# Subtracting the head means from the values instead of from the time mix's output, and a new order of the next stage's first products

## The chip, the cores and the metric

The kernel runs on one core of a Trainium2 chip. The metric is the device time of one execution in microseconds, and lower is better. All data is float32. The large products are split by hand into a high and a low half (`float32r`), so that each costs three passes of TensorE instead of one float32 product.

## The reference, cut to what matters

The program is two decoder layers for 512 tokens with a width of 1024. The change touches one branch of the first, an RWKV-7 time mix with 8 heads of 64 channels:

```python
def step(state, inp):
    r_t, w_t, k_t, v_t, kk_t, a_t = inp
    sa = einsum("bhvk,bhk->bhv", state, kk_t)
    state = (state * w_t[:, :, None, :] - sa[..., None] * (kk_t * a_t)[:, :, None, :]
             + v_t[..., None] * k_t[:, :, None, :])
    return state, einsum("bhvk,bhk->bhv", state, r_t)
...
mean = mean(out, axis=-1)                       # over the 64 channels of a head
var = mean(square(out - mean), axis=-1)
out = (out - mean) * rsqrt(var + GN_EPS) * lnx_w + lnx_b
bonus = sum(rh * kh * r_k, axis=-1) * vh        # with v itself
return (out + bonus) * g
```

The state is zero at first, and every channel v of `state`, `sa` and `out` is linear in the same channel of `v_t`. So if the mean over a head's 64 channels is taken off `v_t`, the output has no mean over them either. The bonus needs `v` as it is.

## The kernel before, in words

The kernel is a row of stages, each a block of five instruction streams (TensorE `pe`, ScalarE `act`, VectorE `dve`, GpSimd `pool`, and SyncE `sp` for DMA). Inside a stage the order of each stream is written out by hand and the streams meet only at semaphores; between stages all of them meet. Activations lie channel by token: a tile is 128 channels (partitions) by 512 tokens. Weights come in groups through two buffers: a DMA, a high part made by ScalarE (`split_hi`, L201), a low part by VectorE (`split_lo`, L209), and then three passes on TensorE (`product`, L232 to L234). An activation tile is split likewise (`Split.hi`, L297, on ScalarE; `Split.lo`, L303 without a gain and L305 with one, on VectorE).

Three stages matter.

The first, `proj_stage`, makes the projections. TensorE goes through 38 weight groups there, and `TimeMixIn.turn` (L499) puts twelve turns in between, two at a time: turns 0 to 3 bring the values `v` to token order, 4 to 7 the keys, 8 to 11 the rates. A turn is four transposes of 128x128 against the constant `ident`; ScalarE copies the result to SBUF.

The third, `time_mix_chunks_stage`, runs the recurrence in four chunks of 128 tokens, with the turned values, and leaves `out` (4 tiles). Its last instructions are a chain of short products and copies (L1201 to L1310).

The fourth, `front_region`, first finishes the time mix (`TimeMixOut`) and then merges three gated branches (`Gates`). The stream of TensorE in it is: `means` (four float32 products with `head_ones`, L1593), `variances` (four float32 products with 8 columns of weights, L1600), and then the loop over steps m = 0 to 35 of the first output tile, with `spread_out` (four float32 products over 8 rows, L1611) ahead of step 10; after that 7 more tiles in a hardware loop. A step is one `product`, so three passes. Steps 0 to 7 need the input tiles x0 to x7 in split form, steps 8 to 11 the branch tiles y0 to y3, steps 12 to 19 x again, steps 20 to 23 need y4 to y7, steps 24 to 31 x, and 32 to 35 need the split output r0 to r3. Nine steps use one weight group.

VectorE's stream at that place is: low parts of x0 and x1; `centre` of the four output tiles (L1624: subtracts the mean that `means` left in PSUM); low parts of x2 to x5; `variance` (L1633); the first `shift` (L1629); `invert` (a reciprocal, L1637, after ScalarE's square root L1620); low parts of x6, x7 and y0 to y3; `split_lo` of the third weight group (which needs step 8 done); and then for each output tile c: `shift`, `finish` (L1642, L1646, L1649), the low part of y(4+c), and the low part of r(c-1). `finish(c)` waits for the c-th product of `spread_out`.

ScalarE's stream: high parts of x0 to x3, four squares of the centred output (L1616), high parts of x4, x5, the square root, high parts of the rest.

Of the kernel before, what the change touches and what calls it, by code (L numbers as in the profile page):

```python
# [8 lines left out]
P = 128  # L9
# [6 lines left out]
NW = W // P  # L16
# [3 lines left out]
HD = 64  # L20
# [14 lines left out]
NEG = -1e30  # L35

ALU = mybir.AluOpType
# [32 lines left out]
for _name, _cols in VECS:  # L70
# [4 lines left out]

CONSTS = [
    ("ident", 128), ("ones", 128), ("head_ones", 128), ("upper", 128), ("causal4", 512), ("neg_tri", 128),
    ("neg_ones", 128), ("neg_diag_t", 128), ("level", 896), ("flip", 128),
    ("causal_add", 128), ("cmp_add", 124), ("cmp_keep", 124), ("head_cols", 32),
]  # L80
CONST_AT = {}
# [313 lines left out]
class TimeMixIn:  # L395
# [94 lines left out]
    def turn(self, pe, u):  # L490
        source, n = (self.v, self.k, self.rate)[u // 4], u % 4
        if u < 4:
            pe.wait_ge(self.bonus_ready, u + 1)
            pe.wait_ge(self.mixed, 14)
        else:
            pe.wait_ge(self.placed, u - 3)
            pe.wait_ge(self.k_made if u < 8 else self.b_made, NW)
        for c in range(NW):
            mm = pe.transpose(self.ps[:, n, c * P:(c + 1) * P], source[:, c, n * P:(n + 1) * P], self.core.c("ident"))  # L499
        mm.then_inc(self.turned, 1)  # L500


# [529 lines left out]
def head_spread(core):  # L1032

    return core.arena[0:HEADS, 70, :]
# [532 lines left out]
class TimeMixOut:  # L1567


    def __init__(self, core, ps):  # L1570
        a = core.arena
        self.core, self.ps = core, ps
        self.out, self.bonus, self.gate = a[:, 8:12, :], a[:, 30:34, :], a[:, 46:50, :]
        self.square, self.rstd = a[:, 56:60, :], a[0:HEADS, 60, :]
        self.spread, self.spread_in = head_spread(core), core.sem("to_spread_in")
        self.mean_banks, self.spread_banks, self.sum_bank = (0, 1, 6, 7), (1, 0, 7, 1), 0
        self.inverted, self.rstd_spread = core.sem("to_inverted"), core.sem("to_rstd_spread")
        self.mean_done, self.centred = core.sem("to_mean_done"), core.sem("to_centred")
        self.squared, self.var_done = core.sem("to_squared"), core.sem("to_var_done")
        self.var_ready, self.rooted = core.sem("to_var_ready"), core.sem("to_rooted")  # L1580
        self.shifted, self.scaled = core.sem("to_shifted"), core.sem("to_scaled")
        self.summed, self.gated = core.sem("to_summed"), core.sem("to_gated")
        self.gate_back, self.bonus_back = core.sem("to_gate_back"), core.sem("to_bonus_back")
# [4 lines left out]
        sp.dma_start(self.spread, self.core.dram["head_spread"]).then_inc(self.spread_in, 16)  # L1588
        sp.wait_ge(self.spread_in, 16)

    def means(self, pe):
        for c in range(NW):
            pe.matmul(self.ps[:, self.mean_banks[c], :], self.core.c("head_ones"), self.out[:, c, :], start=True, stop=True)\  # L1593
              .then_inc(self.mean_done, 1)

    def variances(self, pe):
        pe.wait_ge(self.centred, 1)
        for c in range(NW):
            pe.wait_ge(self.squared, c + 1)
            mm = pe.matmul(self.ps[0:HEADS, self.sum_bank, :], self.core.c("head_cols", c * HEADS, HEADS), self.square[:, c, :],  # L1600
                           start=(c == 0), stop=(c == NW - 1))
        mm.then_inc(self.var_done, 1)

    def spread_out(self, pe):
        pe.wait_ge(self.spread_in, 16)
        pe.wait_ge(self.inverted, 1)
        pe.wait_ge(self.centred, NW)
        for c in range(NW):
            if c == 3:
                pe.wait_ge(self.scaled, 1)  # L1610
            pe.matmul(self.ps[:, self.spread_banks[c], :], self.spread[:, c * P:(c + 1) * P], self.rstd, start=True, stop=True)\  # L1611
              .then_inc(self.rstd_spread, 1)

    def take_square(self, act, c):
        act.wait_ge(self.centred, c + 1)
        act.activation(self.square[:, c, :], self.out[:, c, :], ACT.Square).then_inc(self.squared, 1)  # L1616

    def root(self, act):
        act.wait_ge(self.var_ready, 1)
        act.activation(self.rstd, self.rstd, ACT.Sqrt).then_inc(self.rooted, 1)  # L1620

    def centre(self, dve, c):
        dve.wait_ge(self.mean_done, c + 1)
        dve.scalar_tensor_tensor(self.out[:, c, :], self.ps[:, self.mean_banks[c], :], -1.0 / HD, self.out[:, c, :], ALU.mult, ALU.add)\  # L1624
           .then_inc(self.centred, 1)

    def shift(self, dve, c):
        dve.wait_ge(self.bonus_back, 16)
# [23 lines left out]
class Gates:  # L1652
# [24 lines left out]
    def tensor(self, pe):  # L1677
        core, to = self.core, self.to

        def step(m, d=None):  # L1680
            n, k = m // 12, m % 12
            if k == 0:

                pe.wait_ge(self.pairs_free, n + 1 if d is None else d * 3 + n + 1)
            g = self.g0 + m // 9 + (0 if d is None else 4)
            if m % 9 == 0:
                core.wait_weights(pe, g, 0 if d is None else d - 1)
            if d is None and n == 0 and k < KD:
                pe.wait_ge(self.x_split.lowered, k + 1)
            elif d is None and k >= KD and n < 2:  # L1690
                pe.wait_ge(self.y_split.lowered, 4 * n + k - KD + 1)
            elif d is None and k >= KD:
                pe.wait_ge(to.scaled, NW)
                pe.wait_ge(self.r_split.lowered, k - KD + 1)
            w = core.weights(g, (m % 9) * P, (m % 9 + 1) * P)
            if k < KD:
                mm = product(pe, self.ps[:, 2 + 2 * n, :], w, self.x(k), k == 0, k == KD - 1)
            else:
                mm = product(pe, self.ps[:, 3 + 2 * n, :], w, self.branch(4 * n + k - KD), k == KD, k == 11)
            if m % 9 == 8:  # L1700
                mm.then_inc(core.groups_done, 1)

        to.means(pe)
        to.variances(pe)
        for m in range(36):
            if m == 10:
                to.spread_out(pe)
            step(m)
        with pe.Fori(1, KD) as d:
            for m in range(36):  # L1710
                step(m, d)
        core.used += 32

    def scalar(self, act):
        core, g0 = self.core, self.g0

        def merge(d):
            act.wait_ge(self.summed, 2 * (d + 1))
            act.activation(core.pair(XN_HI, XN_LO, d)[0], self.total[:, d % 2, :], ACT.Copy).then_inc(self.upper, 1)

        def open_up(d, n):
            act.wait_ge(self.logits_ready, 3 * d + n + 1)
            act.activation(self.open_gate[:, n, :], self.open_gate[:, n, :], ACT.Sigmoid, bias=core.v("gate_b", 8 * n + d))\
               .then_inc(self.opened, 1)

        to = self.to
        for k in range(4):
            self.x_split.hi(act, k)
        for c in range(NW):
            to.take_square(act, c)  # L1730
        for k in range(4, 6):
            self.x_split.hi(act, k)
        to.root(act)
        for k in range(6, KD):
            self.x_split.hi(act, k)
        for k in range(KD):
            self.y_split.hi(act, k)
        core.split_hi(act, g0 + 2)
        for c in range(NW):
            act.wait_ge(to.gated, c + 1)  # L1740
            self.r_split.hi(act, c)
            if c == 2:
                core.split_hi(act, g0 + 3)
        open_up(0, 0)
        core.split_hi(act, g0 + 4)
        open_up(0, 1)
        core.split_hi(act, g0 + 5)
        open_up(0, 2)
        for d in range(1, KD):
            for m in range(4):  # L1750
                core.split_hi(act, g0 + 4 * d + m + 2)
                if m:
                    open_up(d, m - 1)
                else:
                    merge(d - 1)
        merge(KD - 1)

    def vector(self, dve):
        core, g0, to = self.core, self.g0, self.to
# [19 lines left out]
                dve.tensor_tensor(total, total, result, ALU.add).then_inc(self.summed, 1)  # L1779

        dve.sem_inc(self.pairs_free, 3)
        for k in range(2):
            self.x_split.lo(dve, k)
        for c in range(NW):
            to.centre(dve, c)
        for k in range(2, 6):
            self.x_split.lo(dve, k)
        to.variance(dve)
        to.shift(dve, 0)
# [1580 lines left out]
def _constants():  # L3370
    c = {name: np.zeros((P, cols), np.float32) for name, cols in CONSTS}
    i = np.arange(P)
    row, col = i[:, None], i[None, :]
# [3 lines left out]
    c["upper"][:] = row <= col  # L3377
    c["causal4"][:] = np.concatenate([row < col, row <= col, row < col, row <= col], axis=1)
    c["neg_tri"][:] = -1.0 * (row >= col)
    c["neg_ones"][:] = -1.0  # L3380
    c["neg_diag_t"][:] = np.where(row < col, 0.0, NEG)
    for n in range(7):
        b = 1 << n
        c["level"][:, n * P:(n + 1) * P] = (col // b % 2 == 1) & (row // b == col // b - 1)
# [95 lines left out]
```

## Time and profile before

| | us |
|---|---|
| median of 3 runs | 2110.09 |
| lowest, highest | 2106.38, 2111.42 |
| profiled execution, from first to last instruction (its span) | 2103.3 |
| TensorE busy in it | 2021.3 |
| VectorE busy | 1079.6 |
| ScalarE busy | 800.6 |
| mean granted TensorE clock, 1 being full | 0.984 |

Of the profiled execution's own time the profile gives the span alone; the lowest run is 3.1 us above that span and the median 6.8 us. The profile shows TensorE busy for 96% of the span; the clock is granted at full speed nearly all of the time. Where such a kernel can gain or lose is in the few places at which TensorE stands idle, does work that could be left out, or runs at half its clock. The stretch that the change touches is small, so the timelines of a few engines over some 40 us say more than the shares of the whole.

### The profile page before, as it was taken

Reading aid. Unit: us, or ns where it says so; the run is one execution under the profiler, and the core shown is the slowest. Engines: PE = TensorE matmul, PEld = TensorE weight load, DVE = VectorE, ACT = ScalarE, POOL = GpSimd, SP = SyncE. Lnnn points to the kernel's source line nnn. Section 1 sums busy time; section 2 is a strip of 40 time slices with the busy share of each in tenths; the row PEclk is TensorE's granted clock in tenths of the full one; section 3 lists DMA queues with packets and bytes.
Section 4 is the critical chain, followed back from the end, with each engine's and each line's share of the span. In section 5 each row is a group of like instructions: output and inputs, shape, how many; then the busy total and the mean of one; then the engine's idle time right before and its main releaser. Section 6 shows DMA issues by size and latency. Waiting matters only on the chain. (4 is left out here: it accounts for less than half of the span.)

```text
span 2103.3 us, 29578 instructions
## 1 busy us (share of the span) xinstructions
PE 2021.3 (96%) x11736; PEld 1611.2 (77%) x11736; DVE 1079.6 (51%) x1815; ACT 800.6 (38%) x1301; POOL 135.1 (6%) x173
## 2 busy tenths in 40 slices
PE   8999879989999998999999999999999999999997
PEld 6778648868888887888888777876666788888886
DVE  5665384464444635577774254238555554423433
ACT  5432342243324424444443232326555544412421
POOL 0000136600000000000000000000000000000000
PEclk9999999999999999999999999999999999999998
DMA  4233200013232430233333423231111222232232
GB/s 177 75 117 113 85 21 3 3 66 116 92 101 91 140 120 13 90 100 98 100 93 110 167 85 105 91 100 51 41 32 40 71 93 90 99 100 92 98 100 80
DMA packets 48594, 181.96 MB, mean 87 GB/s; under 512 B 5504, under 2 KB 5888, under 8 KB 47840
## 3 DMA queue, kind: packets, MB, share of 16 engines
q1 hardware_dynamic: 44240, 165.61, 24.0%
q0 software_dynamic: 3088, 12.90, 1.8%
q10 hardware_dynamic: 1152, 1.89, 0.3%
q8 instruction: 77, 1.26, 0.2%
q14 instruction: 37, 0.30, 0.0%
HBM read 175.08 MB, written 5.29 MB: 86 GB/s over the span
## 5 line engine op out<-in xcount | busy, mean ns | idle before, releaser
L209 DVE TENSOR_TENSOR weights_lo<-weights_raw,weights_hi 128x1024 fp32r<-128x1024 f32 (+2 forms) x288 | 364.4, 1265 | 787.5 <-ACT weights_hi L201 787.3
L201 ACT ACTIVATE weights_hi<-weights_raw 128x1024 fp32r<-128x1024 f32 (+2 forms) x288 | 313.5, 1088 | 836.5 <-PE sp_ps L234 251.1
L232 PE MATMUL sp_ps<-arena_parts,weights_hi 128*128 128x512 f32 x720 | 284.1, 395 | 3.0 <-DVE arena_parts L303 2.5
L234 PE MATMUL sp_ps<-arena_parts,weights_lo 128*128 128x512 f32 x720 | 281.9, 392 | 0.0
L233 PE MATMUL sp_ps<-arena_parts,weights_hi 128*128 128x512 f32 x720 | 281.7, 391 | 0.0
L232 PE MATMUL end_ps<-arena_parts,weights_hi 128*128 128x512 f32 x576 | 224.9, 390 | 0.5 <-DVE arena_parts L305 0.5
L233 PE MATMUL end_ps<-arena_parts,weights_hi 128*128 128x512 f32 x576 | 224.4, 390 | 0.0
L234 PE MATMUL end_ps<-arena_parts,weights_lo 128*128 128x512 f32 x576 | 224.3, 389 | 0.0
L232 PE MATMUL fr_ps<-arena_parts,weights_hi 128*128 128x512 f32 (+1 forms) x480 | 182.3, 380 | 1.9 <-DVE arena_parts L305 1.1
L233 PE MATMUL fr_ps<-arena_parts,weights_hi 128*128 128x512 f32 (+1 forms) x480 | 180.7, 377 | 0.0
L234 PE MATMUL fr_ps<-arena_parts,weights_lo 128*128 128x512 f32 (+1 forms) x480 | 180.7, 376 | 0.0
L232 PEld LDWEIGHTS sp_ps<-arena_parts,weights_hi 128*128 128x128 f32 x720 | 136.1, 189 | 34.4 <-issue 5.3
L233 PEld LDWEIGHTS sp_ps<-arena_parts,weights_hi 128*128 128x128 f32 x720 | 136.0, 189 | 28.6 <-issue 0.7
L234 PEld LDWEIGHTS sp_ps<-arena_parts,weights_lo 128*128 128x128 f32 x720 | 135.9, 189 | 28.4
L232 PEld LDWEIGHTS end_ps<-arena_parts,weights_hi 128*128 128x128 f32 x576 | 108.2, 188 | 23.4 <-DVE arena_parts L305 0.9
L233 PEld LDWEIGHTS end_ps<-arena_parts,weights_hi 128*128 128x128 f32 x576 | 108.2, 188 | 22.7 <-issue 0.2
L234 PEld LDWEIGHTS end_ps<-arena_parts,weights_lo 128*128 128x128 f32 x576 | 108.2, 188 | 22.3
L232 PE MATMUL proj_ps<-arena_parts,weights_hi 128*128 128x512 f32 x272 | 112.0, 412 | 8.9 <-DVE weights_lo L209 8.9
L233 PE MATMUL proj_ps<-arena_parts,weights_hi 128*128 128x512 f32 x272 | 107.4, 395 | 0.0
L234 PE MATMUL proj_ps<-arena_parts,weights_lo 128*128 128x512 f32 x272 | 107.3, 395 | 0.0
L232 PEld LDWEIGHTS fr_ps<-arena_parts,weights_hi 128*128 128x128 f32 x480 | 90.7, 189 | 21.4 <-issue 1.9
L234 PEld LDWEIGHTS fr_ps<-arena_parts,weights_lo 128*128 128x128 f32 x480 | 90.7, 189 | 16.5
(389 smaller groups left out, 3035.6 us busy)
## 6 DMA issues: line engine op xcount, KB each, us to landing
weights_raw<-w_up SPq DMA_DIRECT2D x44, 512.0 KB, 3.5
weights_raw<-w_proj SPq DMA_DIRECT2D x38, 512.0 KB, 3.5
weights_raw<-w_gates SPq DMA_DIRECT2D x32, 576.0 KB, 3.7
weights_raw<-w_ca SPq DMA_DIRECT2D x32, 512.0 KB, 3.5
weights_raw<-w_down SPq DMA_DIRECT2D x16, 704.0 KB, 4.1
weights_raw<-w_in SPq DMA_DIRECT2D x22, 512.0 KB, 3.5
weights_raw<-w_logits SPq DMA_DIRECT2D x16, 512.0 KB, 3.5
weights_raw<-w_ff1a SPq DMA_DIRECT2D x16, 512.0 KB, 3.4
```

Of the source, the lines that this page charges most:

```text
L201: act.activation(self.w_hi[:, g % 2, 0:cols], self.raw[:, g % 2, 0:cols], ACT.Copy).then_inc(self.hi_ready, 1)
L209: dve.tensor_tensor(self.w_lo[:, g % 2, 0:cols], self.raw[:, g % 2, 0:cols], self.w_hi[:, g % 2, 0:cols].bitcast(F32), ALU.subtract).then_ ...
L232: pe.matmul(out, left[0], right[0], start=start, stop=False)
L233: pe.matmul(out, left[0], right[1], start=False, stop=False)
L234: return pe.matmul(out, left[1], right[0], start=False, stop=stop)
```

## The change

Three things are done.

1. A constant `centre` = identity minus `head_ones`/64 takes the place of two unused constants (the constants shrink from 2840 to 2712 columns). Turns 0 to 3 multiply by it with a float32 product in place of a transpose with `ident`, so that the values arrive in token order with their head means gone. `v` in channel order, which the bonus uses, stays as it is.
2. `means`, `centre` and their waits leave `TimeMixOut`.
3. In `front_region` TensorE starts with steps 0 to 3, then come `variances`, steps 4 to 13, `spread_out`, steps 14 to 35. ScalarE interleaves the four squares with the high parts of x1 to x4. VectorE makes the low parts of x0 to x5 without a break.

```diff
 CONSTS:
-    ("neg_ones", 128), ("neg_diag_t", 128), ("level", 896), ("flip", 128),
+    ("centre", 128), ("level", 896), ("flip", 128),
...
 TimeMixIn.turn:
         for c in range(NW):
-            mm = pe.transpose(self.ps[:, n, c * P:(c + 1) * P], source[:, c, n * P:(n + 1) * P], self.core.c("ident"))
+            to, block = self.ps[:, n, c * P:(c + 1) * P], source[:, c, n * P:(n + 1) * P]
+            if u < 4:
+                mm = pe.matmul(to, block, self.core.c("centre"), start=True, stop=True)
+            else:
+                mm = pe.transpose(to, block, self.core.c("ident"))
         mm.then_inc(self.turned, 1)
...
 TimeMixOut:
-    def means(self, pe):
-        for c in range(NW):
-            pe.matmul(self.ps[:, self.mean_banks[c], :], self.core.c("head_ones"), self.out[:, c, :], start=True, stop=True)\
-              .then_inc(self.mean_done, 1)
     def variances(self, pe):
-        pe.wait_ge(self.centred, 1)
...
     def spread_out(self, pe):
-        pe.wait_ge(self.centred, NW)
...
     def take_square(self, act, c):
-        act.wait_ge(self.centred, c + 1)
         act.activation(self.square[:, c, :], self.out[:, c, :], ACT.Square).then_inc(self.squared, 1)
...
-    def centre(self, dve, c):
-        dve.wait_ge(self.mean_done, c + 1)
-        dve.scalar_tensor_tensor(self.out[:, c, :], self.ps[:, self.mean_banks[c], :], -1.0 / HD, self.out[:, c, :], ALU.mult, ALU.add)\
-           .then_inc(self.centred, 1)
...
 Gates.tensor:
-        to.means(pe)
-        to.variances(pe)
         for m in range(36):
-            if m == 10:
+            if m == 4:
+                to.variances(pe)
+            if m == 14:
                 to.spread_out(pe)
             step(m)
 Gates.scalar:
-        for k in range(4):
-            self.x_split.hi(act, k)
+        self.x_split.hi(act, 0)
         for c in range(NW):
+            self.x_split.hi(act, c + 1)
             to.take_square(act, c)
-        for k in range(4, 6):
-            self.x_split.hi(act, k)
+        self.x_split.hi(act, 5)
         to.root(act)
 Gates.vector:
-        for k in range(2):
-            self.x_split.lo(dve, k)
-        for c in range(NW):
-            to.centre(dve, c)
-        for k in range(2, 6):
+        for k in range(6):
             self.x_split.lo(dve, k)
         to.variance(dve)
...
+    c["centre"][:] = c["ident"] - c["head_ones"] / HD
```

## Rows read from the trace of the kernel before

**Rows 1.** The page: one engine's busy time, its share of the span, instructions.

```profile
PE 2021.3 (96%) x11736; PEld 1611.2 (77%) x11736; DVE 1079.6 (51%) x1815; ACT 800.6 (38%) x1301; POOL 135.1 (6%) x173
```

**Rows 2.** Windows: stretch, its length, busy time per engine (instructions), clock, DMA share, GB/s.

```profile
477.60:700.00 222.40, 222.40 (x1012) 185.21 (x1011) 108.07 (x133) 74.57 (x89) 0.00 (x0) 1.00 0.30 96
```

**Rows 3.** Timeline of TensorE, fourth stage: start, length, what; idle before and releaser bracketed.

```profile
435.59 5.85 PE L1593 MATMUL fr_ps<-arena,const_sb 128*128 128x512 f32 x8 [0.95 <-PEq L1093]
441.36 3.60 PE L1600 MATMUL fr_ps<-arena,const_sb 128*8 128x512 f32 x8
...
450.35 0.50 PE L232 MATMUL fr_ps<-arena_parts,weights_hi 128*128 128x512 f32 x1 [1.07 <-DVE arena_parts L305]
...
453.30 3.90 PE L1611 MATMUL fr_ps<-arena 8*128 8x512 f32 x8
457.13 0.80 PE L232 MATMUL fr_ps<-arena_parts,weights_hi 128*128 128x512 f32 x1
...
468.65 0.50 PE L232 MATMUL fr_ps<-arena_parts,weights_hi 128*128 128x512 f32 x1 [0.84 <-DVE arena_parts L303]
...
477.39 0.39 PE L234 MATMUL fr_ps<-arena_parts,weights_lo 128*128 128x512 f32 x1
```

**Rows 4.** Timeline of VectorE, the same stretch.

```profile
436.32 1.41 DVE L305 SCALAR_TENSOR_TENSOR arena_parts<-h,vec_sb,arena_parts 128x512 fp32r<-128x512 f32 x2 [3.50 <-ACT arena_parts L297]
...
446.38 3.34 DVE L1637 RECIPROCAL arena<-arena 8x512 f32<-8x512 f32 x1 [0.31 <-ACT arena L1620]
449.65 1.30 DVE L305 SCALAR_TENSOR_TENSOR arena_parts<-h,vec_sb,arena_parts 128x512 fp32r<-128x512 f32 x2
450.89 2.48 DVE L303 TENSOR_TENSOR arena_parts<-arena,arena_parts 128x512 fp32r<-128x512 f32 x4
453.99 1.36 DVE L209 TENSOR_TENSOR weights_lo<-weights_raw,weights_hi 128x1152 fp32r<-128x1152 f32 x1 [0.62 <-ACT weights_hi L201]
455.26 0.74 DVE L1642 SCALAR_TENSOR_TENSOR arena<-arena,vec_sb,fr_ps 128x512 f32<-128x512 f32 x1
...
464.19 1.29 DVE L303 TENSOR_TENSOR arena_parts<-arena,arena_parts 128x512 fp32r<-128x512 f32 x2
...
467.91 0.69 DVE L303 TENSOR_TENSOR arena_parts<-arena,arena_parts 128x512 fp32r<-128x512 f32 x1
```

**Rows 5.** Timeline of ScalarE, the start of the fourth stage.

```profile
435.56 2.56 ACT L297 ACTIVATE arena_parts<-h,vec_sb 128x512 fp32r<-128x512 f32 x4 [0.29 <-PEq L1093]
438.49 0.63 ACT L1616 ACTIVATE arena<-arena 128x512 f32<-128x512 f32 x1 [0.36 <-DVE arena L1624]
```

**Rows 6.** Timeline of TensorE, the turns (L499) and a run of float32 products (L2067).

```profile
182.13 1.03 PE L499 MATMUL proj_ps_v<-const_sb,arena 128*128 128x128 f32 x8
182.92 0.48 PE L232 MATMUL proj_ps<-arena_parts,weights_hi 128*128 128x512 f32 x1
...
800.20 1.06 PE L2067 MATMUL ca_ps<-arena 128*128 128x128 f32 x8
801.09 1.03 PE L2046 MATMUL ca_ps<-arena 128*128 128x256 f32 x4
```

**Rows 7.** Timeline of TensorE, two resumptions in the second stage.

```profile
259.30 2.16 PE L931 MATMUL sb_ps<-const_sb,arena 128*128 128x128 f32 x8 [4.16 <-DVE arena L1011]
...
279.75 1.65 PE L921 MATMUL sb_ps<-arena 64*128 64x384 f32 x4 [2.12 <-ACT arena L986]
```

**Rows 8.** Windows around clock changes (columns as in rows 2; the clock is third from last).

```profile
259.20:265.80 6.60, 5.71 (x18) 3.07 (x18) 6.60 (x9) 2.72 (x6) 2.16 (x3) 0.50 0.00 0
...
279.50:282.80 3.30, 3.05 (x10) 1.65 (x10) 2.70 (x4) 1.55 (x5) 0.50 (x3) 0.51 0.00 0
...
433.00:440.00 7.00, 6.05 (x22) 3.10 (x23) 2.73 (x4) 3.79 (x6) 0.00 (x0) 0.51 0.47 173
440.00:457.00 17.00, 15.93 (x50) 7.76 (x48) 15.18 (x20) 11.59 (x18) 0.00 (x0) 1.00 0.16 60
457.00:460.50 3.50, 3.50 (x9) 2.70 (x9) 3.43 (x7) 0.63 (x1) 0.00 (x0) 0.51 0.37 140
```

More of the change, by code:

```diff
@@ L1575, in __init__ @@
         self.spread, self.spread_in = head_spread(core), core.sem("to_spread_in")
-        self.mean_banks, self.spread_banks, self.sum_bank = (0, 1, 6, 7), (1, 0, 7, 1), 0
+        self.spread_banks, self.sum_bank = (1, 0, 7, 1), 0
         self.inverted, self.rstd_spread = core.sem("to_inverted"), core.sem("to_rstd_spread")
-        self.mean_done, self.centred = core.sem("to_mean_done"), core.sem("to_centred")
         self.squared, self.var_done = core.sem("to_squared"), core.sem("to_var_done")
@@ L3379, in _constants @@
     c["neg_tri"][:] = -1.0 * (row >= col)
-    c["neg_ones"][:] = -1.0
-    c["neg_diag_t"][:] = np.where(row < col, 0.0, NEG)
+    c["centre"][:] = c["ident"] - c["head_ones"] / HD
     for n in range(7):
```

## The prediction, made before the changed kernel was run

> **What bounds the kernel now.** First the page's line of busy times: TensorE is busy for 2021.3 of 2103.3 us, VectorE for half of that [rows 1]. So what counts is TensorE's stream, and the few places where something else holds it up. Then the windows: from 477.6 us, where the first output tile of the fourth stage ends, to 700 us, TensorE is busy for all of 222.4 us [rows 2]. What this stage gains or loses ahead of 477.6 us is therefore passed on one to one.
>
> Then the timelines of the stage's start. TensorE runs the means for 5.85 us from 435.59 us, most of it at a low clock, then the variances for 3.6 us, then steps 0 to 5, waits 1.07 us for x6, goes on at 450.35, does `spread_out` from 453.30 to 457.1, and once more waits, 0.84 us, at 468.65 for y7 (step 23) [rows 3]. VectorE tells why. From the end of `invert` on (446.38 + 3.34 = 449.7 us) it is the slow one: x6, x7, y0 to y3, the weights' low part, and then from 455.26 us the four `finish` blocks without a break; y7 is ready at 468.6 [rows 4]. So the first tile's end is set by this chain: variances, `variance`, square root, reciprocal, x6 ... step 8, `split_lo`, `finish(0)`, 13.3 us of VectorE up to y7 (455.26 to 467.91 + 0.69 = 468.6), then steps 23 to 35. TensorE's busy share hides this.
>
> **The turns.** Sixteen transposes become sixteen float32 products of 128x128. Eight transposes take 182.92 - 182.13 = 0.79 us, 0.10 each. The same trace shows eight records of float32 products of the same shape in 801.09 - 800.20 = 0.89 us; they are four products of two passes each, so 0.22 us per product [rows 6]. Added: 16 x (0.22 - 0.10) = 2.0 us. TensorE doesn't wait in that stage, so all of it is on the path. It is at least 1.6 us (16 more records at a transpose's 0.10) and at most 2.7 (the row's whole 1.06 us for four products, 0.27 each). I take 2.0, the row's own spacing.
>
> The Trainium skill's page "FP8 and Floating Point Precision" (section "TensorE Precision Notes") says that true FP32 takes four passes through the array. The trace shows two records per product. If each of the four cost a transpose's slot, the turns would cost 16 x 3 x 0.10 = 4.8 us instead of 2.0.
>
> The smaller constants save 64 KB of a load issued behind the first inputs; TensorE's first product waits for a weight, not for it. 0, at most 0.3 us either way.
>
> **The start of the fourth stage.** ScalarE issues high parts and squares at 0.64 us each (2.56 for four) [rows 5]. In the new order x3's high part is the sixth: 435.56 + 6 x 0.64 = 439.4; its low part is ready 0.75 later, 440.15. The fourth square ends at 435.56 + 9 x 0.64 = 441.3. TensorE can begin with step 0 when x0's low part is there, 436.32 + 0.7 = 437.1 [rows 4], so 1.5 us later than it began before. A step costs 0.69 us at the full clock (38 passes from 468.65 to 477.39, 0.23 each [rows 3]) and 1.28 at half. The clock was low up to 440 us, 4.4 us after the means began [rows 3, 8]. Steps 0 to 3 from 437.1 with a rise between 439 and 442.5 end at 441.0 to 442.3. The variances take 3.6 us: done at 444.6 to 446, where they were done at 441.36 + 3.6 = 444.96. So removing 5.85 us of means buys nothing for the chain: four steps fill the place, and they wait for x0 first. I take +0.3 us (bounds -0.4 and +1). VectorE also loses 4 x 0.6 us of centring, ahead of the variances, when it waits anyway: 0.
>
> **From the variances to the first finish.** VectorE still has `variance`, root and `invert` ahead of x6. That chain is unchanged: x6 at 450.3 + 0.3. But of its steps before x6, TensorE has only 4 and 5 left. It is done with them 1.4 us after the variances and then stands still for about 4 us, where it stood 1.07. That alone shifts nothing: step 6 starts when x6 is there.
>
> Then the other edit: `spread_out` comes behind step 13 and not behind step 9. Four steps later is 4 x 0.69 = 2.8 us: it starts at 453.3 + 2.8 = 456.1. The first `finish` waits for its first product (two passes of a 512-column row, 3.9/8 = 0.49 each, and the result's way: about 1.0): 457.1 us. It began at 455.26, released by `split_lo` and not by the spread [rows 4]. So VectorE idles 1.8 us there, and everything behind it (the 13.3 us up to y7, without a break) moves by that. TensorE comes to step 21 at 456.1 + 3.5 + 7 x 0.69 = 464.4, to 22 at 465.1, and waits there for y6 (464.2 + 0.7 + 1.8 = 466.7 [rows 4]), then at step 23 for y7 (470.4): together some 4.9 us, where it waited 0.84. Sum of this edit: +1.8 us (bounds +1.5, +2.2). If the chain were no bound, it would be hidden by those waits.
>
> **The clock.** Each new standstill can cost a spell at half clock. The trace has examples: after 4.16 us of standstill TensorE resumed at 259.30 and ran 6.6 us at half; after 2.12 us it resumed at 279.75 and ran 3.3 at half [rows 7, 8]. The 1.07 and 0.84 of this stage drew none: from 440 to 457 the clock is full [rows 3, 8]. At 457 it fell for 3.4 us right behind `spread_out`, dense as that was [rows 8]; before, the wait at step 23 hid that, and still does. A spell of 3.4 us costs half, 1.7 us, if all of it falls on work. The first, at step 6, delays `spread_out` and so VectorE's chain: I take 1.5. The second, at step 23, delays a TensorE that from there never waits: I take 1.3. Bounds: 0 each, and 3.3 for one like the spell at 259.
>
> **Sum.** 2.0 + 0.3 + 1.8 + 1.5 + 1.3 = +6.9 us. On the profiled execution: a span of 2103.3 becomes 2110.2; the shown median stands 6.8 us above that span, so 2110.1 + 6.9 = 2117.0 us.
>
> **Rivals.**
> - *The waits leave the clock alone* (or the spells fall into the standstills). For: 0.84 and 1.07 us cost nothing. Against: three of the four terms above stay, and the 2.12 us one had its spell. 2.0 + 0.3 + 1.8 = +4.1: 2114.2 us.
> - *TensorE's work sets the end, and the kernel gets faster.* The 5.85 us of means go, the 0.84 us wait and the 1.07 us wait fall out, the turns add 2.0: 2110.1 - 5.85 - 1.9 + 2.0 = 2104.4 us. The place is step 23: it decides if y7 is ready when TensorE gets there, so if `finish(0)` starts at 455.3 or before and VectorE's 13.3 us shrink by 2 or more. The 96% busy share speaks for it; VectorE's row of instructions without a gap, and the wait for y7 already there, against.
> - *One of the spells lasts twice as long*, as at 259: +3.3 on 2117.0, so 2120.3 us. For: a standstill of 4 us like that one; against: it had more gaps behind it.
> - *A float32 turn costs four slots*: 2117.0 + 2.8 = 2119.8 us. It is the rule of the page "FP8 and Floating Point Precision" in the Trainium skill. Against: four products of L2067 in 0.89 us.
> - *The change doesn't do what it says*: were the output not free of its means, no instruction would change; the time is that of the forecast.
>
> **How the numbers follow.** The forecast (both spells) 0.50; no spell or one 0.25; faster by TensorE's work 0.10; a double spell 0.12; four slots 0.03. A measurement of this kernel tells 0.3%, 6.3 us, from no change: the bounds are 2103.8 and 2116.4. The forecast lies 0.6 us beyond the upper one, its own range is 2113.5 to 2119, and I give 0.62 of it to slower and the rest to same; the clock rival is same but for a tenth; the faster one is half faster, half same; the last two are slower. Slower: 0.31 + 0.02 + 0.12 + 0.03 = 0.48; faster 0.05, and one more hundredth for what I don't see; same 0.46. The range for 8 in 10 reaches from 2111.5 to 2120.5: below it lie the faster case and what is left of a small turn cost, above it most of the double spells.
>
> **What would show each step.** Turns: 16 records of L499 in each of two places in place of 8, 1.8 us. Start: step 0 at 437.1 relative to a stage start of 435.6, variances done 9 to 10.4 us after it. First standstill: 3.5 to 4.5 us ahead of step 6, released by L305, and a clock of 0.5 from about there. `finish(0)`: idle ahead of L1642 of about 1.7 us, released by TensorE's L1611. Second: waits for L303 of 4 to 5 us in all. The first tile's end: 42.2 us after the stage start before, 47 after. Wrong would be the prediction if this stretch is shorter than 42.2 us, or if idle ahead of `finish(0)` is none, or if the clock stays full through both waits.

## The result and the profile after

The changed kernel takes 2115.06 us (median of 6 runs, 2109.19 to 2116.45), the kernel before 2108.32 (6 runs, 2105.47 to 2111.42). The ratio is 1.0028, with a 95% interval of 1.0015 to 1.0041: slower by 3 to 9 us. The forecast was 2117.0. A second set of runs (e11, below) gave 2117.14 against 2106.23, ratio 1.0046 (1.0034 to 1.0058). The two intervals overlap between 7 and 9 us. Two single executions far from all the others, one of 2556.55 us of the kernel before and one of 4434.71 us of e9, count in none of the ratios.

The page's busy times answer to [rows 1]: TensorE works 3.0 us longer, in a span that is 9.1 us longer (2112.4 against 2103.3). That is more than the 6.7 us between the medians, and two numbers say why. Wherever a run's time and its core's span are both on record, the time is about 1.8 us above the span. So the profiled execution of the kernel before corresponds to some 2105.1 us, 3.2 under its median, and that of the changed kernel (2114.13 us) to 0.9 under its own.

```profile
PE 2024.3 (96%) x11744; PEld 1615.8 (76%) x11744; DVE 1076.5 (51%) x1811; ACT 800.2 (38%) x1301; POOL 134.8 (6%) x173
```

The timeline of TensorE over the turns answers to [rows 6]. Sixteen records stand for two turns where eight stood; the two pairs start 7.24 us apart, the two transposed pairs behind them 6.33. So a pair of turns costs 0.91 us more, and the four turns 1.8.

```profile
182.66 1.95 PE L501 MATMUL proj_ps_v<-const_sb,arena 128*128 128x128 f32 x16
...
189.90 1.95 PE L501 MATMUL proj_ps_v<-const_sb,arena 128*128 128x128 f32 x16
...
197.15 1.03 PE L503 MATMUL proj_ps_v<-const_sb,arena 128*128 128x128 f32 x8
...
203.48 1.03 PE L503 MATMUL proj_ps_v<-const_sb,arena 128*128 128x128 f32 x8
```

The timeline of TensorE in the fourth stage answers to [rows 3]. ScalarE starts the stage at 440.65 us here, at 435.56 before [rows 5]; times "after the stage's start" are from there.

```profile
442.30 0.77 PE L232 MATMUL fr_ps<-arena_parts,weights_hi 128*128 128x512 f32 x1 [2.58 <-DVE arena_parts L305]
...
447.69 3.70 PE L1597 MATMUL fr_ps<-arena,const_sb 128*8 128x512 f32 x8
451.32 0.50 PE L232 MATMUL fr_ps<-arena_parts,weights_hi 128*128 128x512 f32 x1
...
456.77 0.50 PE L232 MATMUL fr_ps<-arena_parts,weights_hi 128*128 128x512 f32 x1 [3.79 <-DVE arena_parts L305]
...
464.04 3.69 PE L1607 MATMUL fr_ps<-arena 8*128 8x512 f32 x8
467.67 0.50 PE L232 MATMUL fr_ps<-arena_parts,weights_hi 128*128 128x512 f32 x1
...
478.58 0.76 PE L232 MATMUL fr_ps<-arena_parts,weights_hi 128*128 128x512 f32 x1 [2.75 <-DVE arena_parts L303]
...
488.92 0.39 PE L234 MATMUL fr_ps<-arena_parts,weights_lo 128*128 128x512 f32 x1
```

The means (L1593) are gone; in their place are four steps that end at 447.7, all at half clock, and two waits that were 1.07 and 0.84 us are 3.79 and 2.75. VectorE's timeline answers to [rows 4]: `finish(0)` (L1632) waited 2.74 us for `spread_out` (L1607), where it had waited for nothing.

```profile
451.43 0.68 DVE L1623 TENSOR_SCALAR arena<-fr_ps 8x512 f32<-8x512 f32 x1 [4.13 <-PE fr_ps L1597]
...
461.11 1.36 DVE L209 TENSOR_TENSOR weights_lo<-weights_raw,weights_hi 128x1152 fp32r<-128x1152 f32 x1 [1.32 <-ACT weights_hi L201]
465.20 0.75 DVE L1632 SCALAR_TENSOR_TENSOR arena<-arena,vec_sb,fr_ps 128x512 f32<-128x512 f32 x1 [2.74 <-PE fr_ps L1607]
...
477.84 0.68 DVE L303 TENSOR_TENSOR arena_parts<-arena,arena_parts 128x512 fp32r<-128x512 f32 x1
```

The windows show the clock (third number from the end), answering to [rows 8]. Where one spell at half clock stood behind `spread_out`, there are three, and the first low stretch lasts up to 448.

```profile
442.30:448.00 5.70, 5.70 (x13) 3.92 (x14) 3.52 (x5) 5.49 (x9) 0.00 (x0) 0.51 0.86 354
448.00:458.30 10.30, 6.51 (x20) 2.79 (x19) 6.57 (x7) 6.02 (x11) 0.00 (x0) 0.99 0.01 2
458.30:461.70 3.40, 3.40 (x10) 2.65 (x9) 2.08 (x4) 1.17 (x1) 0.00 (x0) 0.52 0.00 0
461.70:468.40 6.70, 6.70 (x22) 3.73 (x21) 3.90 (x7) 0.63 (x1) 0.00 (x0) 1.00 0.27 88
468.40:471.80 3.40, 3.40 (x9) 2.65 (x9) 3.33 (x6) 0.63 (x1) 0.00 (x0) 0.50 0.00 0
471.80:478.50 6.70, 4.03 (x17) 2.75 (x16) 6.56 (x12) 2.23 (x3) 0.00 (x0) 1.00 0.00 0
478.50:481.90 3.40, 3.32 (x8) 2.66 (x9) 3.19 (x5) 1.46 (x3) 0.28 (x1) 0.52 0.28 91
```

Put together, in us after the stage's start (the last column is from the profiles of the experiments):

| | before | after | moved by | from |
|---|---|---|---|---|
| variances done (`variance` starts) | 9.44 | 10.78 | +1.34 | low clock under steps 0 to 3 |
| step 6 starts | 14.79 | 16.12 | +1.33 | nothing new |
| `finish(0)` starts | 19.70 | 24.55 | +4.85 | 1.34 from above, 1.6 half clock (e3), 1.9 place of `spread_out` |
| step 23 starts (y7 ready) | 33.09 | 37.93 | +4.84 | nothing new |
| last pass of step 35 starts (the stretch) | 41.83 | 48.27 | +6.44 | 1.6 half clock behind the wait |

With the turns' 1.8 that is 8.3 us of the 9.1. The rest lies in stretches whose code is the same. The first turn starts 0.5 us later (182.66 against 182.13), the second and third stages took 184.2 us before and 187.0 after, and everything behind the stretch took 1625.9 and 1623.5: 0.5 + 2.7 - 2.4 = 0.8. The same kernel's second profiles (e8, e11) move by as much, so this is scatter. In the second and third stages it goes with the clock. Over the 14 profiles of this text their length and mean granted clock were 184.2 us at 0.95 (the first of the kernel before), 185.8 to 188.2 at 0.91 to 0.93 (ten profiles), and 188.9 to 189.6 at 0.90 (e4, e6, e12).

### The profile page after: what moved, and what is told of

Same layout as the page of the kernel before. It is cut to its first block and busy times, and to the rows that moved or that the text cites. A ratio compares the mean times of both kernels' runs of the same rounds, so it can differ in the third digit from the quotient of the medians.

```text
span 2112.4 us, 29587 instructions
## 1 busy us (share of the span) xinstructions
PE 2024.3 (96%) x11744; PEld 1615.8 (76%) x11744; DVE 1076.5 (51%) x1811; ACT 800.2 (38%) x1301; POOL 134.8 (6%) x173
## 5 line engine op out<-in xcount | busy, mean ns | idle before, releaser
L232 PE MATMUL fr_ps<-arena_parts,weights_hi 128*128 128x512 f32 (+1 forms) x480 | 185.1, 386 | 9.1 <-DVE arena_parts L305 6.4
L233 PE MATMUL fr_ps<-arena_parts,weights_hi 128*128 128x512 f32 (+1 forms) x480 | 183.2, 382 | 0.0
```

Of the source, the lines that this page charges most:

```text
L232: pe.matmul(out, left[0], right[0], start=start, stop=False)
L233: pe.matmul(out, left[0], right[1], start=False, stop=False)
```

## The experiments

The stretch of each is measured as in the table, from one profile each. All are compared with the kernel before in runs beside it, whose medians were 2108.38 for e1 to e4, 2107.81 for e5 to e8, 2108.28 for e9 and e10, 2106.23 for e11 and e12.

**e1 and e12: the turns transposed again.** The means are left out altogether here, so the kernel leaves part of the computation out; the instructions of the fourth stage are those of the changed kernel.

```diff
-            if u < 4:
+            if u < 0:
                 mm = pe.matmul(to, block, self.core.c("centre"), start=True, stop=True)
```

> The changed kernel with turns 0 to 3 as transposes again, the means left out altogether (part of the computation is missing). Theory (turns cost 1.8 us, the rest lies in the fourth stage): the third stage is reached 1.8 us earlier than in the changed kernel, the stretch of the fourth stage up to the last pass of step 35 stays at 48.3 us (41.8 in the kernel before), and the whole is 1.8 us under the changed kernel, some 4 above the kernel before. Rival (the turns cost nothing or four slots a product): 0 or 4.8 us less.

Measured: 2116.7 us (5 runs), ratio 1.0039 (1.0025 to 1.0052). The first pairs of turns start 6.33 us apart and the second stage begins 1.65 us earlier than in the changed kernel, as expected, but the whole isn't shorter. The stretch was 45.4 us and not 48.3, a miss of 2.9 us, which falls into two parts. The clock rose 4.5 us after the stage's start here (0.50 from 437.9 to 444.6 us, 1.00 from 444.7 on) and not 7.4, so the variances came 1.2 us earlier and `variance` started at 9.6; with them the whole chain moved, up to y7 (36.67 and not 37.93). And the spell behind the last wait did not come, that wait being 1.29 us: 1.6 less. The line of the variances in TensorE's timeline:

```profile
446.17 3.60 PE L1597 MATMUL fr_ps<-arena,const_sb 128*8 128x512 f32 x8
```

> e1 once more (turns 0 to 3 as transposes, the means left out altogether), beside the changed kernel on the same chip. Its first five times had a median of 2116.7 us, 1.6 above the changed kernel, though its profile shows the turns 1.7 us shorter. Theory (those five times were scatter from the half-clock spells): 1.8 us under the changed kernel, about 2113. Rival (the transposes make something later slower): at or above the changed kernel again.

Measured: 2117.3 us, ratio 1.0041 (1.0026 to 1.0055), against 1.0046 for the changed kernel beside it; stretch 49.0. The turns save 1.8 us where they stand, and in the time 11 runs of this kernel (mean 2115.9) show nothing of it against 12 of the changed one (2115.5). In the two profiles the second and third stages took 188.2 and 188.9 us; only e4 and e6, with 189.5 and 189.6, took longer in them, and the changed kernel took 187.0 and 185.8. The transposes are not what makes these stages long: e4 and e6 have the products, and the profiles with transposes (the kernel before, e8 and e10 beside these two) reach from 184.2 to 188.9. That points to scatter. But with a standard deviation of some 2.5 us among the runs of each kernel the difference of the two means is known only to about 2 us: the 1.8 us lie at the edge of what the times exclude, and the matter stays open.

**e6: the turns alone,** in the kernel before, with means and centring kept.

```diff
...
+            if u < 4:
+                mm = pe.matmul(to, block, self.core.c("centre"), start=True, stop=True)
+            else:
+                mm = pe.transpose(to, block, self.core.c("ident"))
```

> The kernel before with only the turns 0 to 3 as float32 products with the constant `centre`; means and centring stay and find nothing to take off. Theory: the second stage's first product starts 1.8 to 2.3 us later than before (253.4 us, not 251.3), the fourth stage's stretch stays 41.8 us, the whole is 2 us above the kernel before. Rival (something waits in the first stage that hides them): 251.3 us and no change.

Measured: 2110.78 us (12 runs), ratio 1.0013 (1.0003 to 1.0023), so +0.6 to +4.8 us; the second stage starts at 253.35 us, 71.04 us behind the first turn, where the kernel before took 69.21; stretch 41.6. Here the turns' price does show. Four slots a product are out: the records give 1.8 us, not 4.8.

**e2: spread_out ahead of step 10.**

```diff
-            if m == 14:
+            if m == 10:
                 to.spread_out(pe)
```

> The changed kernel with spread_out ahead of step 10 again and not ahead of step 14. Theory (VectorE's chain from the first finish on sets the end): finish(0) starts some 21.8 us after the stage's start, released by the weights' low part, and not 24.6; with y7 earlier the standstill ahead of steps 22 and 23 shrinks below 1 us and the half clock behind it is gone: stretch 44 us where the changed kernel has 48.3. Rival (TensorE's own work sets the end): moving the same eight passes changes nothing, 48.3 us.

Measured: 2111.86 us (11 runs), ratio 1.0018 (1.0009 to 1.0027), stretch 44.0. TensorE waits 0.19 us at step 23 and `finish(0)` follows `split_lo` without a gap, 21.8 us after the start, in the timeline of VectorE:

```profile
462.30 1.36 DVE L209 TENSOR_TENSOR weights_lo<-weights_raw,weights_hi 128x1152 fp32r<-128x1152 f32 x1 [1.33 <-ACT weights_hi L201]
463.64 0.75 DVE L1632 SCALAR_TENSOR_TENSOR arena<-arena,vec_sb,fr_ps 128x512 f32<-128x512 f32 x1
```

The same work in another place takes 4.3 us off the stretch. 2.7 of them are `finish(0)`, and with it y7, coming earlier: VectorE's chain sets the end. The other 1.6 are the second spell, which doesn't come when the wait at step 23 is 0.19 us.

**e3: the waits filled** with products into an unused bank.

```diff
+        def fill(n):
+            for _ in range(n):
+                product(pe, self.ps[:, 6, :], core.weights(self.g0, 0, P), self.x(0), True, True)
...
+            if m == 6:
+                fill(5)
...
+            if m == 22:
+                fill(1)
+            if m == 23:
+                fill(3)
```

> The changed kernel with more work: 15 extra passes of 128x512 into an unused bank ahead of step 6, 3 ahead of step 22 and 9 ahead of step 23, where TensorE stands still. Theory (each standstill draws a spell at half clock worth 1.5 us): both spells go, the stretch falls from 48.3 to about 45.2 us although TensorE does 27 passes more. Rival (the spells have another cause, or are hidden): 48.3 us or, with 27 x 0.23 us of work on the path, up to 54.5.

Measured: 2114.37 us (7 runs), ratio 1.0029 (1.0017 to 1.0040), stretch 46.4. `finish(0)` starts at 23.1 and not at 24.6: the spell at step 6 is gone, although TensorE did 15 passes more. The variances ended 0.1 us later here than in the first profile of the changed kernel, and as in the second (e11: `variance` at 10.9, `finish(0)` at 24.67); against that one the spell's price is 1.6 us. The spell behind `spread_out` became twice as long (24.5 to 31.5 us after the start), so TensorE reached step 23 without having to wait (37.1, where y7 was ready at 36.4), and part of the second filling lay on the path. The first half of the expectation is shown, the second not; the time doesn't tell e3 from the changed kernel.

**e4: the old order,** without means and centring.

```diff
 TensorE:
+        to.variances(pe)
         for m in range(36):
-            if m == 4:
-                to.variances(pe)
-            if m == 14:
+            if m == 10:
                 to.spread_out(pe)
 ScalarE:
-        self.x_split.hi(act, 0)
+        for k in range(4):
+            self.x_split.hi(act, k)
         for c in range(NW):
-            self.x_split.hi(act, c + 1)
             to.take_square(act, c)
...
```

> The changed kernel with the old order of the fourth stage: variances first, then steps 0 to 9, spread_out, steps 10 to 35, and ScalarE's old order; only the means and the centring are gone. Theory (chain on VectorE, started by the variances): these are done 8.5 to 10 us after the stage's start, where they were done at 9.4, since they now wait for the squares behind x0 to x3; stretch 41 to 42 us against 41.8 before, and the whole is that of the kernel before plus the turns' 1.8 us, less up to 1. Rival (the means' 5.85 us of TensorE were on the path): stretch 36 us, the whole 4 us under the kernel before.

Measured: 2109.24 us (11 runs), ratio 1.0007 (0.9998 to 1.0016), stretch 41.4. TensorE's timeline: it stands idle for 4.06 us up to the first square and takes 5.8 us for the variances, which took 3.6; the two later waits are those of the kernel before.

```profile
446.04 5.81 PE L1597 MATMUL fr_ps<-arena,const_sb 128*8 128x512 f32 x8 [4.06 <-ACT arena L1611]
...
457.23 0.50 PE L232 MATMUL fr_ps<-arena_parts,weights_hi 128*128 128x512 f32 x1 [1.08 <-DVE arena_parts L305]
...
475.53 0.50 PE L232 MATMUL fr_ps<-arena_parts,weights_hi 128*128 128x512 f32 x1 [0.80 <-DVE arena_parts L303]
```

So the loss is the reordering's (TensorE's and ScalarE's together): 6.9 of the stretch. Dropping 5.85 us of means gave 0.4.

**e5: low parts first.**

```diff
 ScalarE:
-        to.root(act)
         for k in range(6, KD):
             self.x_split.hi(act, k)
+        for k in range(3):
+            self.y_split.hi(act, k)
+        to.root(act)
...
 VectorE:
-        for k in range(6):
+        for k in range(KD):
             self.x_split.lo(dve, k)
+        for k in range(3):
+            self.y_split.lo(dve, k)
         to.variance(dve)
...
```

> The changed kernel, with x6, x7 and y0 to y2 made ready by ScalarE and VectorE ahead of the square root and `variance`, in the 4.1 us in which VectorE waits there. Theory: the standstill ahead of step 6 and its spell at half clock are gone, spread_out starts some 17.6 us after the stage's start and not 23.4, finish(0) at about 18.7, the stretch up to the last pass of step 35 is 41 us (48.3 in the changed kernel, 41.8 before), and the whole is near the kernel before, 2108 us. Rival (the order of spread_out and not the standstill is what costs): finish(0) moves by the 1.5 us of the spell alone, stretch 46.7.

Measured: 2111.36 us (12 runs), ratio 1.0014 (1.0005 to 1.0023), stretch 41.6, `finish(0)` at 19.5. The first wait is 0.37 us and no spell follows it. TensorE's steps 6 to 13 no longer stand behind the reciprocal, so `spread_out` starts 5.1 us earlier, although it is still ahead of step 14. It isn't free there: `finish(0)` waits 2.24 us for it, as VectorE's timeline shows, and the spell behind it was a double one (20.8 to 27.5).

```profile
460.02 0.75 DVE L1632 SCALAR_TENSOR_TENSOR arena<-arena,vec_sb,fr_ps 128x512 f32<-128x512 f32 x1 [2.24 <-PE fr_ps L1607]
```

So 6.7 of the changed kernel's 48.3 us go without moving `spread_out`: the order on VectorE and the order on TensorE have to fit each other.

**e8: the kernel before once more.**

> The kernel before once more, for its profile. The second and third stages took 184.2 us in its first profile and 187.0 to 189.5 in those of the changed kernel and its variants, though their code is the same. Theory (the half-clock spells of the second stage fall differently in each execution): this one lies between 184 and 190, with more than 17 us of low clock in the second stage if it is longer. Rival (the centred values or the shifted memory layout make these stages longer): 184.2 again.

Measured: 2107.91 us (12 runs), ratio 0.9993 (0.9984 to 1.0002). Its second and third stages took 187.8 us, at a mean granted clock of 0.91 where the first profile had 0.95 and 184.2 us; its stretch was 41.86. The first profile had been a short one in these stages, and the clock went with it; the stretch repeats to 0.03 us.

**e11: the changed kernel once more.**

> The changed kernel once more, for a second profile and more times. Theory: as before, 2115 us, finish(0) about 24.5 us after the stage's start, a spell at half clock behind each of the two standstills (3.8 and 2.8 us). Its stretch is 48.3 us if both spells fall on work as they did, and between 45.2 and 48.3 us if one falls into a standstill. Rival (the first profile was an odd one): a stretch near 43 and 2110 us.

Measured: 2117.14 us (6 runs); stretch 48.4, `finish(0)` at 24.7, waits of 3.80 and 2.75, `variance` at 10.9. The first profile was no odd one.

**e7: a recut of the fourth stage.**

```diff
 TensorE:
+        to.variances(pe)
         for m in range(36):
-            if m == 4:
-                to.variances(pe)
-            if m == 14:
+            if m == 8:
                 to.spread_out(pe)
 VectorE:
-        for k in range(6):
+        for k in range(5):
             self.x_split.lo(dve, k)
         to.variance(dve)
-        to.shift(dve, 0)
+        for k in range(5, KD):
+            self.x_split.lo(dve, k)
         to.invert(dve)
...
             to.finish(dve, c)
+            if c == 0:
+                core.split_lo(dve, g0 + 2)
```

ScalarE does the four squares first and the shifts as `Identity` with a bias.

> The changed kernel with the fourth stage cut anew: ScalarE squares first, TensorE does the variances first, spread_out ahead of step 8; VectorE makes all x parts ahead of the reciprocal, the shifts go to ScalarE, the weights' low part comes behind finish(0). Theory (VectorE's chain sets the end): variances done 7 to 7.5 us after the stage's start, finish(0) at 15.6, y7 at 29, stretch 38 us against 41.8 before and 48.3 in the changed kernel; with the turns' 2 us the whole is 2106.5, 2 under the kernel before. Rival (TensorE's own work and clock set it): 2 x 3.5 us of small products, 108 passes at 0.23 and 3.4 us lost at half clock give 36 us, so 38 is nearly its floor and a further cut of VectorE would bring nothing.

Measured: 2109.32 us (12 runs), ratio 1.0006 (0.9998 to 1.0015), stretch 41.3, not 38. `finish(0)` came at 14.7, but then VectorE stood still for 4.29 us for the weights' high part, which waits for step 8, and that stood behind a `spread_out` that, mostly at half clock, took 5.7 us. The low clock began 1.4 us after a wait of 1.09 us and lasted from 14.0 to 24.2 us after the start, three times as long as a common spell. VectorE's row:

```profile
461.90 1.36 DVE L209 TENSOR_TENSOR weights_lo<-weights_raw,weights_hi 128x1152 fp32r<-128x1152 f32 x1 [4.29 <-ACT weights_hi L201]
```

**e10: the kernel before, its spread products apart.**

```diff
-            if m == 10:
-                to.spread_out(pe)
+            if m in (10, 13, 16, 19):
+                to.spread_out(pe, (m - 10) // 3)
```

> The kernel before with one edit: the four products of spread_out stand apart, ahead of steps 10, 13, 16 and 19. Theory (in a row they draw a spell at half clock, which the wait at step 23 hides): no low clock follows them, the wait ahead of step 23 grows from 0.8 to about 2.5 us, stretch 41.8 us and time as before. Rival (the spell has nothing to do with them): the low clock is there all the same and the wait stays at 0.8 us.

Measured: 2107.6 us (11 runs), ratio 0.9996 (0.9987 to 1.0005), stretch 41.7. The window has no low clock left, where all 12 other profiles of this text in which the four stand in a row have a spell that begins during them or at most 0.8 us behind them:

```profile
456.00:476.00 20.00, 18.66 (x68) 11.98 (x68) 18.22 (x28) 6.94 (x9) 0.58 (x1) 1.00 0.21 63
```

So the spell comes with the four products in a row. The wait at step 23 grew to 1.34 us and not to 2.5: a product by itself takes 1.05 us of TensorE (456.09 to 457.14) and the passes behind it start 0.1 later, where four in a row took 3.83.

**e9: the recut with its spread products apart.** e7, and spread_out's products ahead of steps 8, 12, 16 and 20; on ScalarE the high parts of the third and fourth weight groups come earlier, and two of the shifts later; and on VectorE:

```diff
-        for c in range(NW):
-            to.finish(dve, c)
-            if c == 0:
-                core.split_lo(dve, g0 + 2)
-            self.y_split.lo(dve, NW + c)
+        core.split_lo(dve, g0 + 2)
+        for c in range(NW):
+            self.y_split.lo(dve, NW + c)
+        for c in range(NW):
+            to.finish(dve, c)
...
```

> The recut kernel (e7) with four more edits: the four products of spread_out stand apart, ahead of steps 8, 12, 16 and 20; ScalarE makes the third weight group's high part ahead of y4 to y7; VectorE makes its low part right after y3; y4 to y7 come ahead of the four finishes. Theory (the 8-row products in a row draw the half clock; VectorE's order and not its work makes TensorE wait at step 23): no low clock behind the first spread product, no wait at step 23, last pass of step 35 some 35.5 us after the stage's start against 41.8 before, 41.4 in e7 and 48.3 in the changed kernel; the whole 2104, 4 us under the kernel before. Rival (a spell at half clock comes anyway, or VectorE's total work of 30 us sets the end): 39 us or more and 2107 or more.

Measured: 2106.23 us (11 runs), ratio 0.9986 (0.9977 to 0.9995), so 1 to 5 us under the kernel before, with the turns' price paid. The stretch is 38.0 us (35.5 expected). Which of its edits brings how much was not run. Placing the products apart brings nothing by itself in the kernel before (e10), and a recut with the means kept was not run either, so that the removal of the means pays here is argued: without them the variances are done 6.3 us after the start, where they were done at 9.4. The timeline of TensorE and two windows:

```profile
442.57 5.23 PE L1597 MATMUL fr_ps<-arena,const_sb 128*8 128x512 f32 x8 [1.61 <-ACT arena L1610]
447.73 0.50 PE L232 MATMUL fr_ps<-arena_parts,weights_hi 128*128 128x512 f32 x1
...
454.44 1.09 PE L1606 MATMUL fr_ps<-arena 8*128 8x512 f32 x2 [0.96 <-DVE arena L1626]
```

```profile
456.00:459.50 3.50, 3.50 (x10) 2.68 (x9) 2.25 (x4) 2.80 (x5) 0.00 (x0) 0.52 0.00 0
460.00:480.00 20.00, 20.00 (x79) 14.27 (x79) 17.59 (x25) 8.65 (x11) 0.58 (x1) 1.00 0.37 123
```

After 455 TensorE never waits; one spell still came, behind a wait of 0.96 us and one 8-row product. Half of its 3.5 us would be 1.7 of the 2.5 us that are missing, which is an estimate.

## Why the prediction was right, and where it was off

The mechanism held: the turns cost a little, removing the means bought nothing, `finish(0)` waited for `spread_out`, and both new standstills drew a spell at half clock. The likeliest case was the one that came. One term was more than four times its forecast, one sign named in advance, the waits for L303, failed, and that the time came out so near is partly luck.

- **Turns.** 2.0 us forecast, 1.8 measured. The FP32 rule in "FP8 and Floating Point Precision" of the Trainium skill (section "TensorE Precision Notes"), counted as four transposes' slots a product, would have given 4.8; the trace contradicts that use of it.
- **Start of the stage.** The term that was mis-sized: +0.3 forecast, with +1 as its bound, +1.34 measured, and +1.45 in e11. The failing step is "steps 0 to 3 from 437.1 with a rise between 439 and 442.5". The clock stayed at half up to 448.0, 7.4 us after the stage's start, where the latest rise allowed was 6.9. Its upper end, 442.3, already holds the case of four steps at half clock (437.1 + 4 x 1.28 = 442.2); the +0.3 took a rise on the way. The missing 0.3 us beyond the bound are step 0 starting 0.1 later than forecast, four steps taking 5.4 and not 5.1, and the variances 3.7 and not 3.6.
- **What that term had left out.** Ahead of step 0 TensorE now stands for 2.58 us at a clock that is low already, where it stood 0.95 ahead of the means, and the low stretch lasted 10.3 us and not 7. Six of the seven profiles with this start have that (`variance` at 10.7 to 11.0); in e1 the clock rose at 4.5 and the term was +0.1. e4, which stood 4.06 us, also has a low stretch of 10 us; e7 and e9, which stood 1.61, have 6.8. That the standstill is the cause is not shown by a run that changes it alone.
- **From the variances to the first finish.** +1.8 forecast for the place of `spread_out`; 4.85 - 1.34 - 1.58 = 1.9 measured. e2 shows that undoing it alone takes 2.7 off `finish(0)` (24.55 to 21.83): the two don't simply add, since with `spread_out` at step 10 only 0.8 of the spell's 1.6 us reach `finish(0)` (21.83 - 19.70 less the later variances' 1.36), through step 8 and `split_lo`.
- **The clock.** 1.5 and 1.3 forecast. e3 against e11 gives 24.67 - 23.09 = 1.58 for the first. For the second, step 23 to the last pass took 10.34 us, against 8.74 before and 8.75 in e1, where a wait of 1.29 us drew none: 1.6.
- **The waits at y6 and y7.** The prediction named "waits for L303 of 4 to 5 us in all" as a sign; it was one wait of 2.75 us, at step 23 alone. The working let TensorE run steps 14 to 20 at the full clock, although the prediction itself has a spell behind `spread_out`: from 467.67 to step 21 it took 6.5 us, not 4.8. It also took 3.5 us for `spread_out`, where the rows give 457.13 - 453.30 = 3.8. Both only shorten a wait, so the sum stands.
- **Sum.** The profiles give 8.3 us in place of 6.9; 1.04 of the difference is the start, 0.3 the second spell. The medians differ by 6.7 us in the first set and by 10.9 in the second (2117.14 against 2106.23). The first interval (3 to 9 us) holds both sums, the second (7 to 12) only the larger.
- **Rivals.** "TensorE's work sets the end": refuted by e4, where 5.85 us less of it gave 0.4. "The waits leave the clock alone": refuted by the windows. "A double spell": not here, though the profiles of e1, e3, e5 and e12 each show one of 6.8 to 7.0 us in this stage, and that of e7 one of 10 us.

The forecast started from a median of 2110.1, which with three more runs became 2108.3: 1.8 us too high, where the sum was 1.4 too low. The two nearly cancelled, and that is luck: 2108.3 + 8.3 is 2116.6, and the two sets gave 2115.1 and 2117.1. The prediction gave 0.48 to "slower" by more than 0.3% and 0.46 to "same". Of the two sets' ratios, 1.0028 and 1.0046, one lies on either side, so the runs don't tell these two apart; that the kernel is slower at all both intervals show.

## What to carry to other kernels

A busy share of 96% does not say that TensorE's work sets the time: look for the stream that runs without gaps up to each wait, here VectorE from the reciprocal to y7. A reorder that fills one hole with steps whose successors still stand behind the same chain moves the hole, and a longer hole costs more than its length if the clock falls behind it. Order the engines' streams together, as e5 and e9 did. e9, which also spreads its small products among dense ones, is the one kernel here that is faster than the one before, by 1 to 5 us; spreading alone (e10) changed nothing that the time shows.

## What the hardware showed that was not expected

Four float32 products over 8 rows in a row, 3.8 us without a gap, are followed by the half clock [rows 3, 8]; the same four, three steps apart, are not (e10, one profile). Four products with 8 columns of weights over 128 rows, 3.6 us, are not followed by it either [rows 3, 8]. A wait of 2.75 us drew a spell in both profiles of the changed kernel and in e12; of the shorter waits those of 0.84, 1.07, 1.25 (e5), 1.29 (e1) and 1.34 us (e10) drew none. Two with 8-row products right behind them did: 0.96 us with one product (e9) and 1.09 with four (e7).
